# A value projection by seven block products, and two modulation blocks streamed later

## The reference, cut to what matters

```python
sh1, sc1, g1, sh2, sc2, g2 = jnp.split(mod[:, None, :], 6, axis=-1)
h = (_rms(x, norm1_g) * (1.0 + sc1) + sh1)
z = h @ w_in                        # 16 column groups of 512, and 20 single columns
y = concatenate([mlstm, moba, retention, nsa]) @ w_out
x = x + g1 * y
h2 = (_rms(x, norm2_g) * (1.0 + sc2) + sh2)
return x + g2 * hier_moe(h2, ...)   # 32 experts of 3 x 2048 x 512
```

## Time and profile before

| | |
|---|---|
| median of 3 runs | 1641.67 us (1641.35 to 1650.01) |
| the profiled execution | 1640.05 us, of it 1638.3 us span |
| granted TensorE clock, mean | 0.905 |
| PE busy | 1379.0 us (84%) |
| DVE busy | 625.7 us (38%) |
| ACT, POOL busy | 191.3, 30.5 us |
| moved by DMA | 611.92 MB, mean 374 GB/s |

### The profile page before, as it was taken

How to read it: one execution, slowest core, us unless ns; L and a number is a source line. 1 busy time by engine, 2 the same in 40 slices (tenths; PEclk the granted TensorE clock), 3 DMA queues, 4 the chain that set the end, 5 groups by cost and what they waited for, 6 DMA issues and landing times.

```text
span 1638.3 us, 18178 instructions
## 1 busy us (share of the span) xinstructions
PE 1379.0 (84%) x7533; PEld 783.3 (48%) x7533; DVE 625.7 (38%) x948; ACT 191.3 (12%) x472; POOL 30.5 (2%) x35
## 2 busy tenths in 40 slices
PE   5999999999999999998787677678767678777767
PEld 4668888678888754663333123123223223223223
DVE  4557783799863555232221121120121121112203
ACT  2002212211112010130100100100101001001001
POOL 0000100000000000010000000000000000000000
PEclk9999999999999999999888788788788778878879
DMA  9997787677856678869999999999999999999997
GB/s 395 428 427 293 294 334 301 255 286 283 336 230 257 256 275 353 359 272 424 428 428 428 428 428 429 428 428 429 429 429 428 428 429 428 429 428 428 428 428 314
DMA packets 44538, 611.92 MB, mean 374 GB/s; under 512 B 4896, under 2 KB 5168, under 8 KB 6736
## 3 DMA queue, kind: packets, MB, share of 16 engines
q1 hardware_dynamic: 42848, 604.00, 88.7%
q0 software_dynamic: 1072, 6.44, 0.9%
q10 hardware_dynamic: 576, 0.89, 0.1%
HBM read 609.21 MB, written 2.10 MB: 373 GB/s over the span
## 4 chain that ended last, share of the span: by engine, by line
DMA 51%; PE 44%; DVE 4%; issue 0%; SPq 0%; ACT 0%; DVEq 0%
DMA ring<-in_exp_w 34%; PE W L688 12%; DMA Zpad<-in_exp_w 9%; PE W L667 7%; DMA ring<-in_stream 5%; PE W L1027 5%; PE M L1119 5%; DMA tail<-in_exp_w 3%; DVE tail L1472 2%; PE W L1003 2%; PE W L675 2%; PE A L1137 2%; PE W L1071 1%; PE M L651 1%; PE W L1084 1%; PE W L641 1%
## 5 line engine op out<-in xcount | busy, mean ns | idle before, releaser
L1472 DVE SCALAR_TENSOR_TENSOR tail<-ring,small,tail 128x512 f32<-128x512 f32 x300 | 225.6, 752 | 10.5
L1119 PE MATMUL M<-ring,g1b 128*32 128x512 f32 x1024 | 148.9, 714 | 64.0 <-DMA ring<-in_exp_w 63.9
L1405 DVE TENSOR_TENSOR consts<-A,tail 32x512 f32<-32x512 f32 x128 | 87.9, 686 | 157.5 <-PE A L1137 154.4
L1983 DVE SCALAR_TENSOR_TENSOR tail<-tail,M 128x128 f32<-128x128 f32 x32 | 9.2, 288 | 297.3 <-ACT tail L1382 297.3
L1091 PEld LDWEIGHTS M<-consts,tail 128*128 128x128 f32 x512 | 69.5, 211 | 94.8 <-ACT tail L1384 61.5
L1137 PE MATMUL A<-Zpad,tail 128*32 128x512 f32 x512 | 86.5, 811 | 31.3 <-DMA Zpad<-in_exp_w 25.8
L667 PE MATMUL W<-buf_h,ring 128*128 128x256 f32 x512 | 111.9, 379 | 0.0
L667 PEld LDWEIGHTS W<-buf_h,ring 128*128 128x128 f32 x512 | 96.7, 190 | 12.9
L1119 PEld LDWEIGHTS M<-ring,g1b 128*32 128x32 f32 x1024 | 30.8, 120 | 147.6 <-DMA ring<-in_exp_w 91.4
L688 PE MATMUL W<-ring,buf_h 128*128 128x256 f32 x432 | 96.7, 380 | 0.0
L1119 PE MATMUL M<-Zpad,g1b 128*32 128x512 f32 x512 | 72.1, 688 | 29.0 <-DMA Zpad<-in_exp_w 29.0
(11 more groups left out here) (317 smaller groups left out, 1339.9 us busy)
## 6 DMA issues: line engine op xcount, KB each, us to landing
ring<-in_stream SPq DMA_DIRECT2D x88, 2048.0 KB, 12.1
ring<-in_exp_w SPq DMA_DIRECT2D x88, 2048.0 KB, 38.4
Zpad<-in_exp_w SPq DMA_DIRECT2D x64, 2048.0 KB, 32.0
PPY<-in_exp_w SPq DMA_DIRECT2D x24, 2048.0 KB, 30.9
tail<-in_exp_w SPq DMA_DIRECT2D x16, 2048.0 KB, 45.2
Zpad<-in_early SPq DMA_DIRECT2D x8, 1536.0 KB, 10.6
buf_x<-in_x SPq DMA_DIRECT2D x2, 1024.0 KB, 6.9
buf_h<-in_x POOLq DMA_DIRECT2D x1, 2048.0 KB, 12.1
```

What stands on the lines that cost most here:

```text
L1119: ins = pe.matmul(M[32 * j:32 * j + 32, 512 * w13:512 * w13 + 512], XT[:, kk, 32 * q:32 * q + 32], w[:, 512 * k:512 * k + 512], start=(kk ...
L1405: return dve.tensor_tensor(o, x, y, op)
L1472: ins = dve.scalar_tensor_tensor(acc, w, cs[:, kk:kk + 1], acc, ALU.mult, ALU.add)
```

## The change

`m_v` joins SEVEN. Its third operand is in `g1b` instead of `pad`, so the load of the bias row into `g1b`, issued by POOL behind product 4 of `n_vw`, is now issued behind product 4 of `m_v`. ACT copies three of its corners in the step `sums_24` and two in the step `chunk`. The modulation blocks behind `m_k` and `m_v` are gone from there: block 12 now comes behind `m_o`, and each later block is two places on, except that a second one (19) stands behind `r_k`, and a third (23) behind n = 2 of the output projection. `ada_rows` and `ada_turn` of blocks 12 to 15 and all `ada_sum` move with their blocks. STREAM has as many items as before, in another order.

```diff
-ADA_BEHIND = {0: N_ADA - 2, 1: N_ADA - 1}
+ADA_BEHIND = {0: N_ADA - 3, 1: N_ADA - 2, 2: N_ADA - 1}
-EARLY_CORNERS = {'n_ks': 3, 'm_o': 2}
+EARLY_CORNERS = {'n_ks': 3, 'm_v': 3, 'm_o': 2}
-SEVEN = ('n_ks', 'n_vs', 'n_kw', 'n_vw', 'm_o', 'b_v', 'r_v', 'b_q', 'b_k')
+SEVEN = ('n_ks', 'n_vs', 'n_kw', 'n_vw', 'm_v', 'm_o', 'b_v', 'r_v', 'b_q', 'b_k')
-         ('chunk', 'm_k'), ('turn', 'n_kw'), ('ada', 12), ('turn_p', 'slc'), ('conv', 'm_k'),
-         ('chunk', 'm_v'), ('ada', 13), ('pv', 'slc'), ('sums_31', 'm_o'), ('sums_24', 'm_o'), ('scores', 'win'),
-         ('chunk', 'm_o'), ('ada', 14), ('sums_31', 'b_v'), ('turn_p', 'win'), ('sums_24', 'b_v'), ('pv', 'win'),
...
+         ('chunk', 'm_k'), ('turn', 'n_kw'), ('sums_31', 'm_v'), ('turn_p', 'slc'), ('sums_24', 'm_v'), ('conv', 'm_k'),
+         ('chunk', 'm_v'), ('sums_31', 'm_o'), ('pv', 'slc'), ('sums_24', 'm_o'), ('scores', 'win'),
+         ('chunk', 'm_o'), ('ada', 12), ('sums_31', 'b_v'), ('turn_p', 'win'), ('sums_24', 'b_v'), ('pv', 'win'),
...
-         ('chunk', 'b_k'), ('ada', 18), ('corners', 'b_k'), ('turn_y', 'm'), ('norm', 'b_k'), ('turn', 'b_k'),
-         ('chunk', 'r_q'), ('scores', 'moba'), ('ada', 19), ('turn_p', 'moba'),
-         ('chunk', 'r_k'), ('pv', 'moba'), ('ada', 20), ('r_scores', 0),
-         ('chunk', 'r_g'), ('r_pv', 0), ('turn_y', 'b'), ('turn_y', 'r'), ('ada', 21)]
+         ('chunk', 'b_k'), ('ada', 16), ('corners', 'b_k'), ('turn_y', 'm'), ('norm', 'b_k'), ('turn', 'b_k'),
+         ('chunk', 'r_q'), ('scores', 'moba'), ('ada', 17), ('turn_p', 'moba'),
+         ('chunk', 'r_k'), ('pv', 'moba'), ('ada', 18), ('r_scores', 0), ('ada', 19),
+         ('chunk', 'r_g'), ('r_pv', 0), ('turn_y', 'b'), ('turn_y', 'r'), ('ada', 20)]
...
-            return g1b[:] if name[0] == 'n' else pad[:, 0:2048]
+            return g1b[:] if name[0] == 'n' or name == 'm_v' else pad[:, 0:2048]
...
-                elif (step, arg) == ('corners', 'n_vw'):
-                    pool.wait_ge(sem["products_done"], products_before('n_vw') + 4)
+                elif (step, arg) == ('sums_24', 'm_o'):
+                    pool.wait_ge(sem["products_done"], products_before('m_v') + 4)
...
                 if step == 'sums_24':
-                    if arg == 'm_o':
+                    if arg == 'm_v':
+                        act.wait_ge(sem["turned"], 1)
+                    elif arg == 'm_o':
                         act.wait_ge(sem["turned"], 2)
```

More of the change, by code:

```diff
@@ L80 @@
          ('chunk', 'm_q'), ('ada', 11), ('cmp_pv', 0), ('scores', 'slc'), ('conv', 'm_q'),
-         ('chunk', 'm_k'), ('turn', 'n_kw'), ('ada', 12), ('turn_p', 'slc'), ('conv', 'm_k'),
-         ('chunk', 'm_v'), ('ada', 13), ('pv', 'slc'), ('sums_31', 'm_o'), ('sums_24', 'm_o'), ('scores', 'win'),
-         ('chunk', 'm_o'), ('ada', 14), ('sums_31', 'b_v'), ('turn_p', 'win'), ('sums_24', 'b_v'), ('pv', 'win'),
-         ('chunk', 'b_v'), ('ada', 15), ('sums_31', 'r_v'), ('m_decay', 0), ('sums_24', 'r_v'), ('turn_y', 'n'),
-         ('chunk', 'r_v'), ('ada', 16), ('sums_31', 'b_q'), ('m_scores', 0), ('sums_24', 'b_q'),
-         ('chunk', 'b_q'), ('ada', 17), ('sums_31', 'b_k'), ('m_pv', 0), ('sums_24', 'b_k'), ('norm', 'b_q'),
+         ('chunk', 'm_k'), ('turn', 'n_kw'), ('sums_31', 'm_v'), ('turn_p', 'slc'), ('sums_24', 'm_v'), ('conv', 'm_k'),
+         ('chunk', 'm_v'), ('sums_31', 'm_o'), ('pv', 'slc'), ('sums_24', 'm_o'), ('scores', 'win'),
+         ('chunk', 'm_o'), ('ada', 12), ('sums_31', 'b_v'), ('turn_p', 'win'), ('sums_24', 'b_v'), ('pv', 'win'),
+         ('chunk', 'b_v'), ('ada', 13), ('sums_31', 'r_v'), ('m_decay', 0), ('sums_24', 'r_v'), ('turn_y', 'n'),
+         ('chunk', 'r_v'), ('ada', 14), ('sums_31', 'b_q'), ('m_scores', 0), ('sums_24', 'b_q'),
+         ('chunk', 'b_q'), ('ada', 15), ('sums_31', 'b_k'), ('m_pv', 0), ('sums_24', 'b_k'), ('norm', 'b_q'),
          ('m_out', 0), ('early', 'b_k'), ('turn', 'b_q'),
-         ('chunk', 'b_k'), ('ada', 18), ('corners', 'b_k'), ('turn_y', 'm'), ('norm', 'b_k'), ('turn', 'b_k'),
-         ('chunk', 'r_q'), ('scores', 'moba'), ('ada', 19), ('turn_p', 'moba'),
-         ('chunk', 'r_k'), ('pv', 'moba'), ('ada', 20), ('r_scores', 0),
-         ('chunk', 'r_g'), ('r_pv', 0), ('turn_y', 'b'), ('turn_y', 'r'), ('ada', 21)]
+         ('chunk', 'b_k'), ('ada', 16), ('corners', 'b_k'), ('turn_y', 'm'), ('norm', 'b_k'), ('turn', 'b_k'),
+         ('chunk', 'r_q'), ('scores', 'moba'), ('ada', 17), ('turn_p', 'moba'),
+         ('chunk', 'r_k'), ('pv', 'moba'), ('ada', 18), ('r_scores', 0), ('ada', 19),
+         ('chunk', 'r_g'), ('r_pv', 0), ('turn_y', 'b'), ('turn_y', 'r'), ('ada', 20)]
 BETWEEN_HALVES = (('gates', 0), ('turn', 'n_q'), ('cmp_scores', 0), ('cmp_pT', 0), ('scores', 'slc'), ('turn_p', 'slc'),
@@ L131, in order_of_pe @@
         elif step not in ('sums_31', 'sums_24', 'corners', 'early', 'm_out', 'norm'):
-            assert not waiting or step == 'conv'
+            assert not waiting or step in ('conv', 'ada')
             placed.append((step, arg))
@@ L1242, in _ @@
                     act.wait_ge(sem["chunk_copied"], chunk_no(arg) - 1)
-                    if arg == 'm_v':
-                        act.wait_ge(sem["turned"], 1)
-                    elif arg == 'r_q':
+                    if arg == 'r_q':
                         act.wait_ge(sem["scores_done"], 2)
```

## The result

| | before | after |
|---|---|---|
| median | 1641.51 us (4 runs, 1641.00 to 1650.01) | 1655.30 us (4 runs, 1654.93 to 1656.53) |
| profiled execution, span | 1640.05, 1638.3 us | 1655.13, 1653.3 us |
| start of the output projection's n = 3 | 678.87 us | 685.70 us |
| from there to the end of the span | 959.4 us | 967.6 us |

The ratio is 1.006, 95% interval 1.0032 to 1.0088. It is smaller than the quotient of the two medians (1.0084): the four runs of the kernel before spread from 1641.00 to 1650.01. Later, against 29 runs of the kernel before, the changed one had a median of 1654.06 (12 runs) to 1644.95, ratio 1.0044 (1.0020 to 1.0067): some 7 us slower.

What follows compares the result with a forecast made beforehand. PE was taken to bound the kernel until about 709 us, then DMA in the expert loop. Terms summed to +6.2 us, step times gave 6.9; +6.5 was carried, giving 1647.8 us, range 1641 to 1653.

Steps and rivals of the forecast that it cites:

- No change: Whole program: time within 0.5% (8.2 us) of the kernel before, chance 0.75.
- The value projection, and its 2.1 us wait for ACT: m_v: one quarter product fewer, -3.45 us; PE idle at product 2 until ACT copies corner 0, +2.1 us.
- The wait ahead of m_o's product 2 goes: m_o: DVE has the third sum ready before PE wants it, so the old wait disappears, -2.31 us.
- Behind b_q: Modulation steps move behind b_k and r_q: wait and half clock go, -4.2 us; new wait behind r_q, +0.65.
- The ring behind r_k: r_g's first load waits for r_k's slot and takes 8.5 us: PE idle +5.0 us, half clock +1.7.
- Inside and behind r_g: Bank A hand-over between two sums +0.9 us; output projection's first load waits for block 19, +4.1, half clock +1.7.
- Block 23 behind n = 2 is free: Output projection: DVE returns before PE asks, n = 3's weights arrive 1.6 us early, cost 0.
- the DMA-bound stretch as long as before: Loop over the experts: its DMA-bound length stays unchanged, so only PE's arrival there shifts the end.
- 2 (the last block's weights late): Output projection n = 3: weights delayed by expert loads issued behind them, +4 us on top, 1652; chance 0.13.
- 3 (the ring does not bite): First halves of r_g and output projection land before PE comes: 1633.8 us profiled, 1635.4 median; chance 0.05.
- 4 (m_v's sums): m_v: DVE late by its convolution, saving of 3.45 us lost, half clock follows: 1651 to 1652; chance 0.05.
- 1, the loads at 7.5 us and the clock that stays up: Both refill waits 1.0 us shorter and no clock falls, 3.4 us off: +1.1, 1642 us; chance 0.17.

Runs made afterwards that it cites:

- reordered corners: One block moved, plus ACT taking m_v's corners 0 and 1 ahead of the turned probabilities, corner 2 in the chunk's step: 1639.90 us, ratio 0.9959 to the kernel before.
- block 19 first: Changed kernel with DVE taking block 19 ahead of its part of r_scores, same stream: 1644.65 us, ratio 0.9986 to the kernel before.
- one block moved: Changed kernel, but block 12 stays behind m_v, later blocks one place on, none doubled behind r_k, b_k's corners earlier: 1638.51 us, ratio 0.9951 to the kernel before.

## Why the prediction was right or wrong

PE's delay was forecast right, 6.5 us against 6.83, and with its parts. The time was not: 1655.3 lies 7.5 us above the 1647.8 and 2.3 above the range. "No change" (within 0.5%), which had 0.75, is undecided: 0.6% in the first runs, 0.44% in the later ones, slower in both.

That 6.5 came so near is in part luck. Up to the end of r_k PE gained 9.2 us (8.6 forecast); behind it the two idle times, the hand-over and the two half clocks cost 14.3 (13.4), and the two misses nearly cancel. The prediction also had two sums, 6.2 by terms and 6.9 by times, and took a middle between them; the one by times was right. Step by step:

- *The value projection, and its 2.1 us wait for ACT*: 1.91, and no fall of the clock behind it. The reordered corners show that it was ACT's order.
- *The wait ahead of m_o's product 2 goes*: gone; product 2 at 351.31, predicted 351.3.
- *Behind b_q*: no wait, no half clock; b_k's first product at 456.23. The new wait behind r_q is 0.55 (0.65 predicted). PE ended r_k at 546.05 (546.6).
- *The ring behind r_k*: 5.13 of wait (5.0), from a load of 8.50 us (8.5). The half clock cost 2.1 in r_g's first half (1.7): it had begun, at 552.0, inside the wait and lasted until 558.9, twice the length of that in the earlier trace rows. The loads of this stream took 8.50 and 8.90 us. By the Trainium skill, DMA: Bandwidth & Descriptors, section on the anatomy of one DMA, an estimate for such a load is 6.8 us, and the wait would have been 3.3. The fit there is told for transfers that GpSimd issues, and SP issued these, which the prediction did not say. The trace differs, and the measurement decides.
- *Inside and behind r_g*: hand-over 0.93 (0.9), second wait 3.92 (4.1), its half clock 1.68 (1.7). The run with block 19 first takes the second wait and its half clock away and leaves the hand-over; the run with one block moved takes both refill waits away.
- *Block 23 behind n = 2 is free*: yes. No wait at L1003, and the 12 idle us of DMA were enough.
- *What failed*: "Every microsecond by which PE reaches that end sooner or later is one for the whole program", and in what would show it, "the DMA-bound stretch as long as before". PE's 6.83 us passed on, but what follows was 8.2 longer. In the first expert group the DMA engines still depend on PE's pace, and with four falls of the clock there the last load landed 5.6 us later than PE's arrival explains; another low stretch, behind that load (the clock was 0.5 from 1637.0 to 1644.5), is most of the other 2.6. The sum had no term for falls behind 715 us: I had read one execution, in which the clock was 1.00 there, and counted clock falls only behind the waits that the change adds. The trace of before could not show the falls; but its mean clock of 0.82 from 780 us on the earlier trace rows, where no wait of PE is over 3.1 us (2.4 in the first group), could have told that they were possible.
- *The base*: four runs of before had a median of 1641.5, with one of 1650.0. Over 29 runs it is 1644.95. The 1650.0 lies inside what those show. With that base the same +6.5 gives 1651.4, against 1654.06 over 12 runs of the changed kernel.

Of the rivals, 2 (the last block's weights late), 3 (the ring does not bite) and 4 (m_v's sums) did not come; of 1, the loads at 7.5 us and the clock that stays up, neither came.

What stays open: what decides in a given execution whether the clock falls in the first group, and whether the change makes that more frequent. The changed kernel had four falls in both its traces, the kernel before in one of two; that is too few to tell.

## What to carry to other kernels

In a ring that is filled in stream order, moving an item to a place with slack on the engine that reads it can still stall another engine: ask for each item which one held its slot, and when that is released. Two items of one consumer in a row make the load behind them wait for the last item of the other consumer; here one moved block gained 0.5% and two lost as much. And compare spans only after comparing the granted clock of the stretch in which the next bound is still being filled: there PE's clock becomes the program's time, and one profiled execution may show only one of two outcomes.

## What the runs showed of the hardware

The same kernel, idle for the same 2.7 to 3.1 us behind b_q, had half clock afterwards for 3.4 us in two executions and for 13.7 in a third (460.5 to 474.2, in a stretch of small matmuls); in the first expert group with the same gaps it had none in one and four falls in another, and from n = 3 to the end these took 959.4 and 966.9 us. A wait of 5.13 us brought a low clock that began inside the wait and lasted 6.8 us; after a wait of 4.66, in the run with block 19 first, it lasted 3.4. With matmuls that nobody reads in two of the gaps no fall was seen in that group in the one trace, and ten runs stayed within 5.6 us where they otherwise spread over 8.5. The version with fillers, one block moved and the corners reordered (1638.0), and the plain one with one block moved (1638.5), are faster than both kernels; against the kernel before by 0.45% and 0.49%.
